# Modulation weights by output feature: a product along a row on GpSimd, a sum along the free axis on ScalarE, in place of sums over partitions

## What is computed

```python
def adaln_params(cond, w, b):                       # cond: (1, 1024), w: (1024, 6144)
    mod = jax.nn.silu(cond) @ w + b
    return jnp.split(mod[..., None, :], 6, axis=-1)

sh1, sc1, g1, sh2, sc2, g2 = adaln_params(c, mod_w[i], mod_b[i])
h_lat = modulate(rmsnorm(x, norm_g[i, 0]), sh1, sc1)          # h * (1 + sc1) + sh1
x = x + g1 * hyena_mix(h_lat, p)
x = x + g2 * conv_ffn(modulate(rmsnorm(x, norm_g[i, 1]), sh2, sc2), ...)
```

## Time and profile before

| | us |
|---|---|
| median of 3 runs | 1064.82 (1064.22 to 1065.75) |
| span of the profiled execution | 1061.4 |
| TensorE busy in it | 1042.7 |
| GpSimd busy | 542.9 |
| VectorE busy | 667.8 |
| ScalarE busy | 418.1 |

### The profile page before, as it was taken

How to read it: one execution, slowest core, us unless ns; L and a number is a source line. 1 busy time by engine, 2 the same in 40 slices (tenths; PEclk the granted TensorE clock), 3 DMA queues, 4 the chain that set the end, 5 groups by cost and what they waited for, 6 DMA issues and landing times.

```text
span 1061.4 us, 13502 instructions
## 1 busy us (share of the span) xinstructions
PE 1042.7 (98%) x4984; PEld 858.3 (81%) x4984; DVE 667.8 (63%) x1007; ACT 418.1 (39%) x687; POOL 542.9 (51%) x401
## 2 busy tenths in 40 slices
PE   7999999999999999999999999999999999999996
PEld 5889887777878888778888888778888888888885
DVE  5663766766499665995788847386666656520603
ACT  6223557665554243644344432442323223221222
POOL 1688895999200064234344345535465545553541
PEclk9999999999999999999999999999999999999999
DMA  6446454342446922212222113303222232223222
GB/s 256 164 168 228 130 191 149 91 161 70 179 159 248 379 91 99 103 57 80 94 83 86 54 51 150 142 37 140 99 80 79 95 142 79 79 80 132 106 80 79
DMA packets 18567, 131.92 MB, mean 124 GB/s; under 512 B 2369, under 2 KB 2769, under 8 KB 11986
## 3 DMA queue, kind: packets, MB, share of 16 engines
q1 hardware_dynamic: 8784, 92.62, 23.3%
q0 software_dynamic: 6560, 27.27, 8.0%
q10 hardware_dynamic: 3170, 11.30, 2.8%
HBM read 124.89 MB, written 6.29 MB: 124 GB/s over the span
## 4 chain that ended last, share of the span: by engine, by line
PE 95%; DVE 2%; ACT 1%; issue 0%; DMA 0%; POOL 0%; POOLq 0%; ACTq 0%; DVEq 0%
PE bank L505 81%; PE bank L496 7%; PE bank L511 3%; PE bank L752 1%; PE bank L746 1%; PE bank L904 1%; PE bank L741 1%; PE bank L561 1%; DVE arena L2186 0%; DMA small<-small_in 0%; DVE arena L2189 0%; PE bank L913 0%; PE bank L753 0%; PE bank L869 0%; ACT arena L1202 0%
## 5 line engine op out<-in xcount | busy, mean ns | idle before, releaser
L1738 POOL TENSOR_TENSOR ring_parts<-ring,ring_parts 128x1024 fp32r<-128x1024 f32 x102 | 247.9, 2435 | 266.8 <-ACT ring_parts L1202 264.1
L505 PE MATMUL bank<-hT_parts,ring_parts 128*128 128x512 f32 x1344 | 339.2, 393 | 0.8 <-ACT hT_parts L1531 0.8
L1202 ACT ACTIVATE ring_parts<-ring 128x1024 fp32r<-128x1024 f32 (+2 forms) x163 | 168.4, 1042 | 383.6 <-PE bank L505 220.6
L505 PEld LDWEIGHTS bank<-hT_parts,ring_parts 128*128 128x128 f32 x1344 | 249.6, 188 | 54.7 <-ACT hT_parts L1531 2.4
L505 PE MATMUL bank<-ring_parts,hT_parts 128*128 128x512 f32 (+1 forms) x672 | 171.5, 379 | 1.0 <-POOL ring_parts L1738 0.6
L505 PE MATMUL bank<-ring_parts,arena_parts 128*128 128x512 f32 (+1 forms) x736 | 172.4, 386 | 0.0
L505 PEld LDWEIGHTS bank<-ring_parts,arena_parts 128*128 128x128 f32 x736 | 136.6, 188 | 27.9 <-DVE arena L2424 0.3
L505 PE MATMUL bank<-arena_parts,ring_parts 128*128 128x512 f32 x592 | 148.0, 391 | 0.3 <-DVE arena_parts L2293 0.3
L505 PEld LDWEIGHTS bank<-ring_parts,hT_parts 128*128 128x128 f32 x672 | 122.4, 188 | 22.8 <-POOL ring_parts L1738 1.0
L2530 DVE SCALAR_TENSOR_TENSOR arena<-bank,small,arena 128x441 f32<-128x441 f32 (+2 forms) x176 | 122.3, 695 | 23.8 <-DVE arena L2525 0.3
L505 PEld LDWEIGHTS bank<-arena_parts,ring_parts 128*128 128x128 f32 x592 | 111.0, 188 | 25.5 <-DVE arena_parts L2293 2.1
(11 more groups left out here) (227 smaller groups left out, 1106.5 us busy)
## 6 DMA issues: line engine op xcount, KB each, us to landing
ring<-weights_in SPq DMA_DIRECT2D x39, 2048.0 KB, 8.0
arena<-mod_w_in POOLq DMA_DIRECT2D x32, 512.0 KB, 4.2
arena<-mod_w_in POOLq DMA_DIRECT2D x8, 1024.0 KB, 5.5
x_sb<-x_in SPq DMA_DIRECT2D x4, 512.0 KB, 5.6
...
```

The costliest lines, as they stand in the source:

```text
L505: ins = nc.tensor.matmul(out, l, r, start=start and n == 0, stop=stop and n == len(passes) - 1)
L1202: return nc.scalar.activation(out, in_, ACT.Copy)
L1738: return nc.gpsimd.tensor_tensor(part(low), low, part(high), ALU.subtract)
```

## The change

The matrix is laid out the other way: a tile has 128 output features on partitions and the 1024 input features along the free axis, so that one partition's sum is one output number. There are 48 such tiles (6 rows of 8), all loaded by GpSimd's queue into four buffers in turn (at 99, 103 and 65 KB of `arena`, and the second half of `mod_g`). `silu(c)` now stands as a whole row of 1024 numbers on all partitions (`cond_row`, the first half of `mod_g`): SP loads it with a broadcast ahead of three small loads and chunk DK, and ScalarE takes the silu of 128 x 1024 in place of 128 x 8. GpSimd multiplies each tile by that row, two full tiles as inputs, and does nothing else on it. ScalarE sums each along the free axis: a copy with an accumulator (`mod_sums`), at places that a table names (`MOD_BY_PIECE`) and at six others. GpSimd issues the load of tile j + 3 after its product j, when ScalarE's sum j - 1 is done.

The first loads no longer wait for `lambda_sums` but for chunk DK. The latent roots now follow product 34, the roots of the four heads follow the last product. The wait for the probabilities is gone. TensorE's `modulation` and `gate_rows`, VectorE's `mod_chunk`, the spill and the copies of the gate rows are gone. VectorE's bias addition moves from about 449 us to the end of the attention. The gates go to memory as 2048 single numbers and come back as rows on all partitions, two DMAs of ScalarE's queue between the gates and the merge. The transform tables are loaded earlier, since no modulation sums stand in their place.

```diff
-MOD_POOL_COLS = 128
-MOD_AFTER = (9, 11, 13, 15, 16, 17, 18, 19)
-ROOTS_AFTER = (11, 21, 23, 25, 27)
-PAUSE_AFTER = 17
+MOD_TILES = 6 * KD
+MOD_BUFFERS = 4
+LATENT_ROOTS_AFTER = 34
+MOD_BY_PIECE = {4: (0, 0), 5: (0, 0), 6: (0, 3), 7: (3, 7), 8: (7, 8), 9: (8, 10), 10: (10, 12), 11: (12, 15), 12: (15, 16),
...
 # SP
+            sp.dma_start(cond_row, cond_d.partition_broadcast(P).rearrange("p a d -> p (a d)")).then_inc(sem("cond_in"), 16)
             sp.dma_start(rowed, rowed_d).then_inc(sem("constants_in"), 16)
...
 # TensorE
-            modulation(0)
-            gate_rows(0)
             wo_tile(0)
             wo_tile(1)
-            modulation(1)
-            gate_rows(1)
             filter_tile(0)
             wo_tile(2)
-            modulation(2)
             filter_tile(1)
...
             wo_tile(7)
-            gate_rows(2)
-            gate_rows(3)
-            modulation(3)
...
 # ScalarE
-            nc.scalar.activation(st(CSILU, KD), small[:, SMALL["cond"]], ACT.Silu).then_inc(sem("cond_ready"), 1)
+            wait("cond_in", 16)
+            nc.scalar.activation(cond_row, cond_row, ACT.Silu).then_inc(sem("cond_ready"), 1)
...
+            def mod_sums(first, end):
+                for j in range(first, end):
+                    wait("mod_scaled", j + 1)
+                    w = modw[j % MOD_BUFFERS]
+                    nc.scalar.activation(w, w, ACT.Copy, accum_out=modc[:, j:j + 1]).then_inc(sem("mod_summed"), 1)
+
             for p in range(4, 15):
                 split_high(p)
+                mod_sums(*MOD_BY_PIECE[p])
             for i in range(8, 12):
                 input_out(i)
+            mod_sums(18, 21)
             for i in range(4):
                 qk_out(i)
...
             for i in range(4, 8):
                 qk_out(i)
+            mod_sums(32, 36)
             for k in range(KQ):
                 split_high(FIRST_UQ + k)
+                mod_sums(36 + k, 37 + k)
...
             dgate_out(3)
+            mod_sums(39, 43)
             split_high(FIRST_UKV)
             for h in range(HEADS):
                 wait("latq_done", TT + h + 1)
                 nc.scalar.activation(qn[:, h, :], bank[4 + h], ACT.Identity, scale=-MLA_SCALE).then_inc(sem("qn_out"), 1)
+                mod_sums(43 + h, 44 + h)
             split_high(FIRST_UKV + 1)
+            mod_sums(47, 48)
...
 # GpSimd
-            wait("lambda_sums", 1)
-            load_pool(0)
-            load_pool(1)
+            chunk_landed(pool, C_DK)
+            for j in range(MOD_BUFFERS - 1):
+                load_mod(j)
             wait("cond_ready", 1)
...
+            for j in range(MOD_TILES):
+                w = modw[j % MOD_BUFFERS]
+                wait(f"modw_in{j % MOD_BUFFERS}", 16 * (j // MOD_BUFFERS + 1))
+                nc.gpsimd.tensor_tensor(w, w, cond_row, ALU.mult).then_inc(sem("mod_scaled"), 1)
+                if j + MOD_BUFFERS - 1 < MOD_TILES:
+                    if j:
+                        wait("mod_summed", j)
+                    load_mod(j + MOD_BUFFERS - 1)
+                if j == LATENT_ROOTS_AFTER:
                     latent_roots()
```

168 lines of the change are left out of this document (41 added, 127 removed).

## The result

| | before | after |
|---|---|---|
| median, us | 1065.28 (4 runs, 1064.22 to 1065.85) | 1125.44 (4 runs, 1123.26 to 1128.38) |
| span of the profiled execution, us | 1061.4 | 1121.3 |
| TensorE busy, us | 1042.7 | 1056.9 |
| mean granted clock of TensorE | 0.998 | 0.975 |

The ratio is 1.0572, with a 95% interval from 1.0559 to 1.0584. Slower was forecast, at 1105; the time lies 10 us above the range that ends at 1115, and 8 above the 1117 to which the bounds of the terms reached.

The account below looks back on a forecast made before the run. TensorE's work was taken as the bound. GpSimd's calendar added 44 us ahead of scores(0), the clock 2, less 5.4 gained: +40.6 on a span of 1061.4 gives 1102.0, plus 3.4 for the median: 1105.4; range 1064 to 1115.

Parts of the forecast that it names:

- What bounds the kernel, and the sign: Whole kernel: the sum of TensorE's work sets the time; the change makes it slower, chance 0.83.
- A tile: GpSimd, per modulation tile: product 2.40 us, load 0.57 in series, gap 0.08, together 3.05 us.
- VectorE in the way: Projections: some 20 VectorE subtractions lengthen GpSimd's work by 13 us, between 4 and 24.
- Where GpSimd waits: Loads on GpSimd waiting for ScalarE's sums: blocks of 7.7 us at the start and 6 at load 36.
- Load 36: GpSimd's load 36 waits for sum 32 behind ScalarE's squares and qk_out: a block of 6 us, between 0 and 8.
- The path to `scores(0)`: First scores: product 47 ends at 199.6 us, then its sum and ScalarE's copies; scores(0) at 202.8, +44 us.
- Where the stalls show: TensorE waits at chunk LAT0, about 21 us, released by ScalarE's qk_out; the rest at the latents and scores.
- TensorE's gain: Removed column sums, merge and output tiles: TensorE sheds 10.4 us and keeps 5.4, between 4.3 and 10.4.
- the clock: TensorE after a stall: one start at a lower clock costs 2 us, between 0 and 4.
- GpSimd is never late below 2.63 us a tile: Rival for GpSimd's work up to the latent keys: TensorE hardly waits, 1064.6 us, 1059.4 to 1070; chance 0.20.
- Hidden issues: Rival on GpSimd: load issues run beneath products, or products are cheap; 1085.5 us, between 1075 and 1095; chance 0.22.

Follow-up runs that it names:

- e1: The changed kernel with one wait more: GpSimd waits for the end of its own product before issuing the next load; 1125.3 us.
- e6: The changed kernel with the modulation tiles' loads from the fifth on issued on ScalarE's queue instead of by GpSimd; 1102.1 us.
- e7: The changed kernel with GpSimd's products over 832 of the 1024 columns of a tile; 1121.0 us.
- e5: The changed kernel with modc padded to 96 columns, so arena starts 256 bytes behind its place in the kernel before; 1118.7 us.
- e3: The changed kernel with the products and the sums over 16 of the 1024 columns of each tile; 1067.0 us.

## Why the prediction was wrong, step by step

- **What bounds the kernel, and the sign: right.** TensorE's work is the time; the loss is made ahead of `scores(0)`, and there by the new work on GpSimd.
- **A tile: right.** 2.40 us for the product (measured 2.41), 0.57 for the load (0.60), serial: a product starts 0.02 us behind its issue's end. The first product was to be at 25.5 and was at 26.38.
- **VectorE in the way: the first half of the step that failed.** The prediction took from the earlier trace rows that a subtraction lengthens GpSimd's instruction and put 13 us on GpSimd. GpSimd lost about 1. VectorE lost 53 us of its own (143.9 busy instead of 91.0), most of it locked out behind issues, and TensorE waited for it: 32.5 us under L1849 and L1960, the 7.6 us to 207.47 among them. The earlier trace rows had a part of it, 2.92 us for an instruction that takes 1.22 alone; the prediction priced GpSimd's side and never asked what it is on VectorE's. That the lockout would make it worse no row before could say: there GpSimd waited 0.3 us for its own last addition before an issue, and e1 shows that such a gap lets VectorE in. In e6, without the issues, the forecast term is there as it was worked out: 48 products take 127.8 us instead of 115.7, 12 more.
- **Where GpSimd waits: the second half, and the term that was mis-sized.** 7.7 + 6 us for ScalarE and nothing for data were forecast; 31.0 and 10.5 came, 27.8 us too little in the sum, of which the wrong 13 hid almost half. The six waits for ScalarE are 6.8 us at the start, 5.3 at load 36, and four that weren't listed, of 3.5, 3.0, 2.7 and 9.7 us. The last stands behind sum 39 and VectorE's 14.8 us at the latents: VectorE waits for GpSimd, TensorE for VectorE, ScalarE for TensorE, and GpSimd for ScalarE. Such a ring was not in the sum, which took each wait by itself from where the rows stood before. How much of the 27.8 the lockout caused isn't shown: without it, in e1, the waits are 15.4 us shorter, but GpSimd's row is 14.6 longer, and e7 shows that the waits move against the row's length even with the lockout in place (19.3 us less of products, 12.6 more of waits).
- **Load 36: a right number from a wrong one.** The prediction has product 33 end at 138.6. That leaves 1.7 us for VectorE, where product 20 had been given 6 already; with 6 the block would have come out at 1.7 us, not 6. That 5.3 were measured is luck.
- **The path to `scores(0)`: right, and nearly overtaken.** Product 47, its sum and the copies were to set the date, 3.2 us behind the product. The copies end 3.1 us behind it; TensorE, held up by VectorE until 207.47 and then slow by its clock, needed 0.6 us more.
- **Where the stalls show: half right.** They were to stand at `qk_out`, the latents and the scores, and do. But the releasers are VectorE's rows, where ScalarE's `qk_out` had been named.
- **Missing: the start of arena.** 6.7 us by e5. The width of `modc` stood in the diff of the full kernel and the tile that aligns `arena` in the code; nothing in the prediction looks at addresses. With it the sum would have been 1112. The alignment has 6.5 us in the second block and 0.6 ahead of 383.
- **TensorE's gain: right, the clock by luck.** Up to the last output tile 4.8 us were forecast as kept and 4.8 came (57.64 less 52.86). Behind it 0.6 of 3.4 were forecast; TensorE won 2.3 and gave 2.1 back in the wait for VectorE's scaling, which doesn't come earlier by what TensorE gained. The 2 us for the clock were meant for some start after a stall; 1.4 were lost in this one place, in four of the twelve runs that have the wait.
- **The rivals.** That GpSimd is never late below 2.63 us a tile did not arise: with everything in it a tile took 3.9 us, and 3.7 in e7. Shorter products alone (e7) didn't get there, so it stays untested. Hidden issues were to give 1085. They aren't hidden, and the nearest to that case is e6, whose issues stand on ScalarE's queue: `scores(0)` is at 194, not 177 to 183, as VectorE takes the 12 us there and GpSimd waits 33.5 us for data. e3 shows the bottom of it: without the work 1067.0, and by e5 some 1060 with `arena` in its place. So the change could have won 4 to 5 us, if the work were free; this is an estimate from 1067.0, less the 6.7 of e5, against 1064.9.

Summed at TensorE's last product: 12.4 us on GpSimd's calendar, 0.5 at its end, 7.1 for the address, less 0.2 in the gain, 19.9 in all. The end of the span is 0.7 us less behind than that product, and the median stands 4.1 us above the span instead of 3.4; these two cancel, and 1125.4 less 1105.4 is 20.0.
